# Experts' stage of a two-layer model: gathers of four heads by 32 tokens, weighted sums in four column groups

## The reference

```python
def peer_ffn(h, w_q, sub_keys, u, v):
    q = (ht @ w_q).reshape(T, PEER_HEADS, 2, PEER_DKEY // 2)      # 8 heads, two halves of 128
    s = jnp.einsum('thpc,hpnc->thpn', q, sub_keys)                # 128 keys a half
    v1, i1 = lax.top_k(s[:, :, 0], K); v2, i2 = lax.top_k(s[:, :, 1], K)     # K = 16
    cand = (v1[..., :, None] + v2[..., None, :]).reshape(T, PEER_HEADS, K * K)
    cand_idx = (i1[..., :, None] * PEER_NKEYS + i2[..., None, :]).reshape(T, PEER_HEADS, K * K)
    top_s, pos = lax.top_k(cand, K)
    idx, g = jnp.take_along_axis(cand_idx, pos, axis=-1), jax.nn.softmax(top_s, axis=-1)
    # for each token, head and k: two rows of 1024 out of 16384
    a = jnp.einsum('thkd,td->thk', jnp.take(u, ib, axis=0), xb)
    w = jax.nn.gelu(a) * gb
    return jnp.einsum('thk,thkd->td', w, jnp.take(v, ib, axis=0))

x = x + peer_ffn(rmsnorm(x, norm_ffn[i]), ...)
g_ple = jax.nn.sigmoid(rmsnorm(x, norm_ple[i]) @ ple_gate[i])     # the gated projection
x = x + g_ple * (p[i] @ ple_proj[i])
```

## Time and profile before

| | |
|---|---|
| three runs | 3353.21, 3357.67, 3358.05 us (median 3357.67) |
| span of the profiled execution | 3353.7 us; its own time is not given beside it |
| experts' stage (first gather issued to last copy of a sum) | 575.5 to 1907.1 us |
| gathers issued by GpSimd | 512 |
| TensorE busy over the span | 91% |
| VectorE, ScalarE, GpSimd busy | 62%, 22%, 20% |
| DMA over the span | 240 GB/s, 803.37 MB |

### The profile page before, as it was taken

The page is one execution under the profiler, slowest core; times in us unless marked ns, Lnnn a source line. Parts: engine busy times, 40 slices in busy tenths (PEclk is TensorE's granted clock), DMA queues, the critical chain, the costliest instruction groups (busy, mean ns, idle before and its releaser), DMA issues. The chain is left out here.

```text
span 3353.7 us, 31224 instructions
## 1 busy us (share of the span) xinstructions
PE 3067.3 (91%) x11456; PEld 1759.1 (52%) x11456; DVE 2070.2 (62%) x4483; ACT 754.6 (22%) x1661; POOL 664.3 (20%) x649
## 2 busy tenths in 40 slices
PE   9999899988988788788888889999999998999998
PEld 3554544433333333344443445448854476878887
DVE  6577823776777777677676438437567777466423
ACT  2144211322222222222222221112111143121000
POOL 1210001444444444444444200000000000000000
PEclk9999999999999989899999999999999999999999
DMA  6774212999999999999999632112245464122222
GB/s 213 256 240 144 76 63 105 422 421 421 421 421 418 420 418 420 417 415 416 410 422 417 283 133 76 38 66 88 84 171 212 184 238 154 63 76 88 88 88 76
DMA packets 119545, 803.37 MB, mean 240 GB/s; under 512 B 13824, under 2 KB 16384, under 8 KB 32352
## 3 DMA queue, kind: packets, MB, share of 16 engines
q0 software_dynamic: 91312, 619.09, 45.8%
q1 hardware_dynamic: 28080, 182.28, 15.1%
HBM read 771.96 MB, written 29.36 MB: 239 GB/s over the span
## 5 line engine op out<-in xcount | busy, mean ns | idle before, releaser
L1354 PE MATMUL po<-pair,diag 128*128 128x512 f32 x2048 | 983.8, 637 | 176.8 <-ACT diag L1453 176.7
L1576 DVE SCALAR_TENSOR_TENSOR pair<-pair,h_tm 128x1024 f32<-128x1024 f32 x512 | 618.9, 1225 | 329.5 <-DMA pair<-in_peer_uv,idx 323.3
L1354 PEld LDWEIGHTS po<-pair,diag 128*128 128x128 f32 x2048 | 409.8, 204 | 718.0 <-issue 480.5
L1215 POOL DMA_INDIRECT pair<-in_peer_uv,idx x512 | 591.5, 1155 | 918.8 <-PE po L1354 671.5
L1446 ACT ACTIVATE ge<-a 128x2 f32<-128x2 f32 (+2 forms) x178 | 36.4, 204 | 919.7 <-DVE pair L1576 915.7
L1996 PE MATMUL acc<-a,ring 128*128 128x512 f32 x512 | 220.9, 592 | 0.0
L1453 ACT ACTIVATE diag<-ident,wt 128x128 f32<-128x128 f32 x512 | 169.1, 392 | 41.0 <-DVE wt L1580 40.8
L1996 PEld LDWEIGHTS acc<-a,ring 128*128 128x128 f32 x512 | 97.3, 190 | 122.0 <-issue 122.0
L1707 PE MATMUL bank<-hT,weight_sums 128*128 128x256 f32 x592 | 139.8, 379 | 0.0
L1707 PE MATMUL bank<-hT,ring 128*128 128x256 f32 x592 | 139.8, 379 | 0.0
L1683 DVE TENSOR_TENSOR weight_sums<-ring 128x512 f32<-128x512 f32 x53 | 36.7, 692 | 165.9 <-DMA ring<-in_w_fc 150.0
(11 more groups left out here) (504 smaller groups left out, 4110.0 us busy)
## 6 DMA issues: line engine op xcount, KB each, us to landing
ring<-in_w_fc SPq DMA_DIRECT2D x62, 1024.0 KB, 4.8
mg<-in_ada_w POOLq DMA_DIRECT2D x96, 512.0 KB, 5.1
tab<-s_tables SPq DMA_DIRECT2D x16, 1664.0 KB, 6.4
ring<-in_w SPq DMA_DIRECT2D x15, 1024.0 KB, 4.8
first<-in_w_first SPq DMA_DIRECT2D x14, 1024.0 KB, 7.8
other<-in_w_first SPq DMA_DIRECT2D x14, 1024.0 KB, 6.3
s_tables<-weight_sums POOLq DMA_DIRECT2D x8, 1664.0 KB, 6.6
s_tables<-table POOLq DMA_DIRECT2D x8, 1664.0 KB, 6.1
```

The lines of the kernel that those rows point to most:

```text
L1215: pool.indirect_dma_start(out=pair[:, at, :], out_offset=None, in_=core.dram["peer_uv"][:, :], in_offset=bass.IndirectOffsetOnAxis(ap=idx[ ...
L1354: last = pe.matmul(po[:, t % 2, half * 512:(half + 1) * 512], diag[:, at, :], pair[:, at, D + half * 512:D + (half + 1) * 512], start=firs ...
L1576: dve.scalar_tensor_tensor(row, row, 1.0, h_tm[:, t, :], ALU.mult, ALU.mult, accum_out=a[:, s:s + 1]).then_inc(dotted, 1)
```

## The change

A unit is now four heads by 32 tokens of one tile: partition 32 h + i holds token i of the quarter for head h of four. A tile has eight such units (four quarters `j` by two halves of the heads), and the list SUPERS gives the order of (tile, half of the heads): the tiles come in turn, only the first two are mixed, tile 3 is last. A group is four gathers, one from each quarter, except at the start (the first four groups take them from one or two quarters) and at the very end. What follows from the new layout:

- A weight diagonal is 128 x 32 (`spread`, four small identities on top of each other, times the weights). The product with it adds the four heads and gives 32 rows, so the four quarters of a group go to four column groups of TensorE and four partition ranges of `po`. `used` counts groups, not gathers, and the four slots of a group become free together. RING is 9, and 8 for the first 16 groups.
- The turned rows are needed four times over, one below the other (`h_rows`): `tokens` makes them with 32-column products, 32 for each quarter.
- `score` is eight products of 32 columns. The first unit needs four heads, so eight blocks of the projection for tile 0 instead of two (`project_first`), and weight chunks 1 to 3 are loaded at the stage's start, before the first gather. The remaining blocks for the other tiles stand behind the groups 0, 1 and 4 to 11.
- The picks are cut into four parts, spread over the groups by `pick_times`.
- Tiles 0 to 2 are finished before tile 3's last units, so the gated projection of 384 tokens stands beside tile 3, one feature block a group, and `ple` does the last 128 tokens.

```diff
-UNITS = TT * PH
-RING, EARLY, GRP, AHEAD = 11, 10, 4, 2
-LAST_PROJECT = 11
...
+SUPERS = [(0, 0), (1, 0), (0, 1), (1, 1), (2, 0), (2, 1), (3, 0), (3, 1)]
+QUAD, TOK = 4, 32
+RING, EARLY = 9, 8
+DONE = 3 * P
...
+def sequence():
+    first = [[(0, 0), (0, 1), (0, 2), (0, 3)], [(0, 4), (0, 5), (1, 0), (1, 1)], [(0, 6), (0, 7), (1, 2), (1, 3)],
+             [(0, 8), (0, 9), (1, 4), (1, 5)]]
+    first += [[(0, 10 + i), (1, 6 + i), (2, i), (3, i)] for i in range(6)]
+    first += [[(1, 12), (2, 6), (2, 7), (3, 6)], [(1, 13), (2, 8), (3, 7), (3, 8)], [(1, 14), (2, 9), (2, 10), (3, 9)],
+              [(1, 15), (2, 11), (3, 10), (3, 11)], [(2, 12), (2, 13), (3, 12), (3, 13)], [(2, 14), (2, 15), (3, 14), (3, 15)]]
+    out = [[(0, j, s) for j, s in group] for group in first]
+    for su in range(1, len(SUPERS)):
+        out += [[(su, j, s) for j in range(QUAD)] for s in range(PK)]
+    return out[:-1] + [out[-1][0:2], out[-1][2:3], out[-1][3:4]]
+def pick_times():
+    counts = {-1: 8, 0: 4, 1: 4}
+    counts.update({3 + i: 1 + i % 2 for i in range(11)})
+    todo = [(u, part) for u in range(QUAD * len(SUPERS)) for part in range(4)]
+    times, g = {}, -1
+    while todo:
+        n = counts.get(g, 1 if g >= 14 else 0)
+        times[g], todo = todo[:n], todo[n:]
+        g += 1
+    return times
...
-    for n in range(UNITS * PK):
-        if n == (LAST_PROJECT + 1) * PK:
+    for g, group in enumerate(groups):
+        if g == PK:
             queue = [(s, -1) for s in range(EARLY, RING)] + queue
-        s, before = queue.pop(0)
-        filled[s] += 1
-        found.append((s, before, filled[s]))
-        queue.append((s, n))
+        for _ in group:
+            s, before = queue.pop(0)
+            filled[s] += 1
+            found.append((s, before, filled[s]))
+            queue.append((s, g))
...
-def groups(unit):
-    if unit <= LAST_PROJECT:
-        return [(s, 2) for s in range(0, PK, 2)]
-    if unit < UNITS - 1:
-        return [(s, GRP) for s in range(0, PK, GRP)]
-    return [(0, 4), (4, 4), (8, 4), (12, 2), (14, 1), (15, 1)]
...
+        diag = st.sb("diag", [P, 3, QUAD, TOK])
...
+        late = 2 * PK * 3
+        project_at = {g: 8 + g - 4 for g in range(4, 12)}
+        tokens_at = {start + 2 * j: (t, j) for t, start in ((1, 6), (2, 3 * PK + 2), (3, 4 * PK + 2)) for j in range(QUAD)}
+        out_at = {3 * PK: 0, 4 * PK: 1, late: 2}
+        back_at = {3 * PK + 2: 0, 4 * PK + 2: 1, late + 1: 2}
+        lift_at = {late + 6 + n: n for n in range(KT)}
+        next_at = late + PK
...
+            for c in range(1, 4):
+                sp.dma_start(ring[c], w[c * P:(c + 1) * P, :]).then_inc(w_landed[c], 16)
+            for c, free in ((4, 2), (5, 8), (6, 10), (7, 12)):
+                sp.wait_ge(made, free)
+                sp.dma_start(ring[held[c]], w[c * P:(c + 1) * P, :]).then_inc(w_landed[held[c]], 16)
...
             def project_rest(i):
-                pe.wait_ge(first_taken, i + 1)
+                if i < 2:
+                    pe.wait_ge(first_taken, i + 1)
+                else:
+                    pe.wait_ge(taken, i - 1)
...
+            def score(u):
+                t, g = SUPERS[u // QUAD]
+                if u < QUAD:
+                    pe.wait_ge(first_taken, 2)
                 else:
-                    pe.wait_ge(first_taken, 2)
-                if unit >= 1:
-                    pe.wait_ge(sc_ready, unit)
+                    pe.wait_ge(taken, 8 * g + 8)
+                if u:
+                    pe.wait_ge(sc_ready, u)
                 for q in range(2):
-                    last = pe.matmul(ps[:, q, :], qT[:, 2 * h + q, t * P:(t + 1) * P], keys[:, 2 * h + q, :], start=True, stop=True)
+                    for hh in range(QUAD):
+                        i, some = 2 * (QUAD * g + hh) + q, slice(t * P + u % QUAD * TOK, t * P + (u % QUAD + 1) * TOK)
+                        last = pe.matmul(ps[hh * TOK:(hh + 1) * TOK, q, :], qT[:, i, some], keys[:, i, :], start=True, stop=True,
+                                         skip_group_check=True)
...
+            def tokens(t, j):
                 for half in range(2):
-                    if t or half:
-                        pe.wait_ge(copied, 2 * t + half)
+                    n = 2 * (QUAD * t + j) + half
+                    if n:
+                        pe.wait_ge(copied, n)
                     for k in range(4):
-                        last = pe.transpose(pt[:, k * P:(k + 1) * P], core.hT[:, half * 4 + k, t * P:(t + 1) * P], ident[:, :])
+                        some = core.hT[:, half * 4 + k, t * P + j * TOK:t * P + (j + 1) * TOK]
+                        for hh in range(QUAD):
+                            last = pe.matmul(pt[hh * TOK:(hh + 1) * TOK, k * P:(k + 1) * P], some, ident[:, :], start=True, stop=True,
+                                             skip_group_check=True)
...
+            for i in range(8):
+                project_first(i)
             pe.wait_ge(tables, 32)
             score(0)
-            tokens(0)
-            project_rest(0)
-            project_rest(1)
+            for j in range(QUAD):
+                tokens(0, j)
             score(1)
...
             score(2)
-            for unit in range(UNITS):
-                t, h = place(unit)
...
-                for s0, size in groups(unit):
-                    for s in range(s0, s0 + size):
-                        n = unit * PK + s
-                        first = h == 0 and s == 0
-                        if first and t >= 2:
-                            pe.wait_ge(tile_out, 2 * t - 2)
-                        pe.wait_ge(diag_ready, n + 1)
-                        at = slot[n][0]
...
-                        last.then_inc(used, 1)
-                    end = s0 + size
-                    if unit <= LAST_PROJECT and end in (4, 8):
-                        project(unit + 4, end // 4 - 1)
-                    if end == 12 and unit + AHEAD + 1 < UNITS:
-                        score(unit + AHEAD + 1)
...
+            for i in range(4):
+                project_rest(i)
+            score(3)
+            begun = set()
+            for g, group in enumerate(groups):
+                for i, (su, j, s) in enumerate(group):
+                    t = SUPERS[su][0]
+                    if t >= 2 and (t, j) not in begun:
+                        pe.wait_ge(tile_out, 2 * t - 2)
+                pe.wait_ge(diag_ready, starts[g] + len(group))
+                for half in range(2):
+                    for i, (su, j, s) in enumerate(group):
+                        t, quad = SUPERS[su]
+                        at = slot[starts[g] + i][0]
+                        last = pe.matmul(po[j * TOK:(j + 1) * TOK, t % 2, half * 512:(half + 1) * 512], diag[:, g % 3, i, :],
+                                         pair[:, at, D + half * 512:D + (half + 1) * 512],
+                                         start=((t, j, half) not in begun), stop=(quad == 1 and s == PK - 1), skip_group_check=True)
+                        begun.add((t, j, half))
+                        begun.add((t, j))
+                last.then_inc(used, 1)
+                if g in (0, 1):
+                    project_rest(4 + 2 * g)
+                    project_rest(5 + 2 * g)
+                if g in project_at:
+                    project(project_at[g])
+                for u in score_after(g):
+                    score(u)
+                if g in tokens_at:
+                    tokens(*tokens_at[g])
+                if g in back_at:
+                    turn_back(back_at[g])
+                if g == late + 3:
+                    sums_done()
+                if g in lift_at:
+                    gate(lift_at[g])
+                    lift(lift_at[g])
...
+            take_first(0)
+            take_first(1)
             score(0)
-            tokens(0)
-            for i in range(2):
-                act.wait_ge(made, i + 1)
-                act.activation(qT[:, i, P:S], acc[:, i, P:S], ACT.Copy).then_inc(taken, 1)
+            for j in range(QUAD):
+                tokens(0, j)
+            score(1)
             exponentials(0)
-            score(1)
+            score(2)
+            take_rest(0)
+            take_rest(1)
...
+                size = len(group)
+                act.wait_ge(dotted, starts[g] + size)
+                act.activation(ge[:, g % 4, 0:size], a[:, g % 4, 0:size], ACT.Gelu_apprx_tanh).then_inc(gelu_done, 1)
+                act.wait_ge(wt_ready, g + 1)
+                if g >= 3:
+                    act.wait_ge(used, g - 2)
+                for i in range(size):
+                    act.activation(diag[:, g % 3, i, :], spread[:, :], ACT.Copy, scale=wt[:, g % 4, i:i + 1]).then_inc(diag_ready, 1)
+                if g in (0, 1):
+                    exponentials(2 + g)
+                    take_rest(4 + 2 * g)
+                    take_rest(5 + 2 * g)
+                if g in project_at:
+                    project(project_at[g])
+                for u in score_after(g):
```

(10 more changed lines are left out.)

404 lines of the change are left out of this document (190 added, 214 removed).

## The result

The changed kernel takes 3430.09 us (median of 4 runs, 3423.53 to 3436.31), the one before 3355.44 (3351.18 to 3358.05): a ratio of 1.0221, 95% interval 1.0202 to 1.0241. Its profiled execution has a span of 3429.5 us, 75.8 more than before. 3417 was predicted, in a range of 3366 to 3480.

A forecast was written before the change was run, and what follows sets the result against it. Bound: the gather stream's start, moments without a gather under way, and what follows the last landing. 12.4 - 5.0 + 34 + 34 + 0 - 2 - 14 = +59.4 us: span 3413.1, median 3417, range 3366 to 3480.

The forecast's parts named there:

- Start (+12.4): First gather issued 12.4 us later, needing eight projected blocks, not two; two chunk loads moved to free DMA time give -5.0.
- terms 2 and 3: DMA idle in the first groups (+34 us) and in groups 4 to 11 (+34 us).
- Groups 0 to 11 (+34 and +34): First groups wait behind turned rows, scores and 384-column blocks; groups 4 to 11 behind 512-column blocks; +34 us each.
- term 3: Groups 4 to 11: gelu, diagonals, sum, block and copy form one closed loop, longer than four gathers' 9.96 us; +34 us.
- Groups 12 to 127 (0): Nine slots cover the chain to the next issue; picks and gated blocks (8.7 us a group) are also covered; 0 us.
- Tail (-2 and -14): After the last gather: shorter last sum on an empty TensorE, -2 us; gated projection of 128 tokens, not 256, -14 us.
- terms 1, 2 and 5: Later first gather (+12.4, chunk loads -5.0), idle DMA in the first groups (+34), shorter tail (-2 and -14 us).
- The stream ran dry: Forecast of DMA gaps early in the experts' stage; its rival, a stream never dry, gave 3349 us, chance 0.12.
- the column groups overlap: Forecast of 1.7 us for a 16-record sum; its rival, no overlap, kept 6.9 us and gave 3477 us, chance 0.06.
- the loop is not hidden: Forecast that groups 4 to 11 cost +34 us; its rival, that loop hidden but not the start, gave 3383, chance 0.06.
- Nine slots do not run short: Forecast for groups 12 to 127; its rival, nine slots too few, added 120 us and gave 3537 us, chance 0.08.
- the rival's price: With too few slots and 10.1 us landings, a group takes 11.0 us, not 9.96; +120 us over 112 groups, chance 0.08.

The follow-up runs named there:

- copy_later: The changed kernel with ScalarE's copy of each projected block (groups 4 to 11) moved behind the next group's diagonals; 3429.10 us, ratio 1.0228.
- gate_gaps: The changed kernel with a free group after every second gated block beside tile 3, giving the weight chunk time to land; 3430.66 us, ratio 1.0233.
- tail_256: The changed kernel with the gated projection of 256 tokens beside tile 3 and 256 after the last gather, as before the change; 3452.61 us, ratio 1.0295.

## Why the prediction was right, and where not

- **Start (+12.4).** 13.5 and 11.2 in the two profiles. The first issue is at 589.02, 587.9 was forecast. The chunk loads taken off the stream (-5.0, and those counted inside terms 2 and 3) show as some 10 of the -16.6 us of groups 16 to 101.
- **Groups 0 to 11 (+34 and +34).** From group 1 to group 16 the issues lose 81.4 us; less four chunk loads that went ahead, 10.0, it is 71.4, against 34 + 34 - 5 = 63 forecast: 8 too little. The first sum began at 619.22 (620 forecast). The eight loops, from sum 4 at 683.15 to sum 12 at 806.20, take 123.1 us, as forecast (111 + 12), but part of that is luck: four are shorter than their own sums in term 3 and four longer, by 6 us each way. The longest, that of group 10, was put at 20.3 us and took 21.8. Its sum and the next one were counted like the others but took 5.32 and 5.14 us, where a sum over four quarters took 3.64 at half clock: `sequence` gives these groups two gathers from one quarter, and products of one quarter follow one another, as in group 0 (7.05 us for 16 records). And the loop has more links than its formula: by copy_later the score and the turned rows close it as well as the block's copy.
- **Groups 12 to 127 (0).** This step failed, by its sentence "also covered" on the gated blocks: +20.0 in groups 102 to 111, of which 2.9 came back later and 5.0 are two chunks that used to travel earlier, so some 12 us lost. I had counted 8.7 us of products against 9.96 and not the chunk that must come through the full queue into a single buffer. gate_gaps (105.3 us there) shows the wait, tail_256 (109.1) the products. For the other groups it holds: four column groups overlap, 1.92 us for 16 records at full clock and 3.64 at half, as forecast (1.7 and 3.4).
- **Tail (-2 and -14).** -2.3 and -14.9, with 0.7 more between them; and 3.8 that were not forecast between the last issue and the last dot (+95.4 and +91.6 above).
- **Sum.** 59.4 forecast, 75.8 measured on the span, 16.4 more: some 12 from the gated blocks, the rest from the first groups, less what the tail gave. The mechanism of terms 1, 2 and 5 is shown by the traces, that of term 3 in part; that the gated blocks still fell within the range is owed to its width, for no term stood for them.
- **Rivals.** The stream ran dry as forecast (rate 44 GB/s in 620 to 630), the column groups overlap, the loop is not hidden. Nine slots do not run short; eight do, at the rival's price.

The granted clock was 0.62 from 991 to 1639 us in the changed kernel against 0.92 from 900 to 1557 before; a sum took 3.64 us there, and the stream lost nothing by it (418 GB/s in both). In the loops of groups 4 to 11 it did cost time: after 5 us of idling the sum of group 5, at 700.19, took 3.64 us and its block 8.34, after 1.92 us of idling those of group 6, at 714.60, took 1.92 and 7.13; the 1.5 us a loop of the forecast stood for this. The Trainium skill says in "TensorE: Matmul & The Clock Gate", section "HAM oscillation — how this bites in real kernels", that bursts between waits for DMA start throttled each time. The trace agrees on the clock; on the time it agrees only where the sum is not covered. The Trainium skill also says in "TensorEngine Tiling (Array Packing)", section "Tiling Modes", that a change of tiling mode drains the engine. If it does, little shows: the 16 records of the sum that starts at 1736.10 are followed by a full-array block 1.85 us later, at 1737.95, and at the prediction's 0.107 us each they need 1.7.

## What to carry to other kernels

When slots are freed in groups and work is queued behind each group's sum, look at every engine that has to act once before the next sum, and at everything in its queue there. Put whatever waits for slow work behind the next group's urgent work, all of it and on all engines. Closing one gap is worth little while another copy or another engine still closes the loop; the groups' issue times side by side show at once where a gain has gone. And take an idea out of a large change and try it alone in the old layout: the last tile's order was worth 0.5% by itself.

## What had not been expected of the hardware

- The same program differed by 12 us (3430.09 and 3442.08) between two sets of runs, while the kernel before differs by 1.7 (3355.44 and 3357.18). In the slower one ScalarE idles for up to 6.9 us, 41.8 in all, ahead of copies of turned rows whose input TensorE had finished (the first at 593.94, after 6.03 us). Its cause was not found, nor whether it makes the 12 us: copy_later has 37.3 us of it at 3429.10.
- One slot of nine is worth 1.0 us a group of 10.1, with the DMA engines' busy share all but unchanged (0.97 against 1.01): the share does not tell a full queue from one that is short; the rate does (376 against 413 GB/s from 950 to 1000 us).
